# Last layer of heads of a four-layer kernel: the rotated rows moved by small transfers from ScalarE in place of swap products on TensorE, and the products half a product further ahead

## What is computed

```python
h = rmsnorm(x, attn_norm[layer])                  # x: 256 x 1024
proj = h @ w_in_odd[i]                            # 1024 x 3072
mq, mk, mv = jnp.split(proj, 3, axis=-1)          # each 16 heads of 64
mq = apply_partial_rope(mq.reshape(B, S, 16, 64), cos, sin)
mk = apply_partial_rope(mk.reshape(B, S, 16, 64), cos, sin)
moba_out = moba_attention(mq, mk, mv)             # softmax(causal(q k^T / 8)) v, per head
x = x + moba_out.reshape(B, S, 1024) @ w_out_odd[i]

def apply_partial_rope(t, cos, sin):              # rotates the first 16 of 64 features
    half = 8
    t1, t2 = t[..., :8], t[..., 8:16]
    rot = concatenate([t1 * cos - t2 * sin, t2 * cos + t1 * sin])
    return concatenate([rot, t[..., 16:]])
```

## Time and profile before

| | us |
|---|---|
| Three runs, median (lowest to highest) | 1150.59 (1150.18 to 1150.71) |
| The profiled execution, its time | 1150.78 |
| The profiled execution, its span | 1148.9 |
| TensorE busy (matmuls) | 1133.4, 99% |
| Weight loads of TensorE busy | 963.1, 84% |
| VectorE busy | 829.4, 72% |
| ScalarE busy | 654.8, 57% |
| GpSimd busy | 130.8, 11% |
| Traffic | 206.55 MB, 180 GB/s in the mean |

### The profile page before, as it was taken

One profiled execution on the slowest core, in us unless ns is written; L12 is line 12 of the kernel. 1 busy time (PEld: TensorE's weight loads), 2 busy tenths in 40 slices (PEclk: granted clock), 3 DMA queues, 4 the chain that ended last, 5 costly groups with the idle time before them and its releaser, 6 DMA issues.

```text
span 1148.9 us, 26306 instructions
## 1 busy us (share of the span) xinstructions
PE 1133.4 (99%) x10447; PEld 963.1 (84%) x10447; DVE 829.4 (72%) x1345; ACT 654.8 (57%) x1026; POOL 130.8 (11%) x168
## 2 busy tenths in 40 slices
PE   9999999999999999999999999999999999999998
PEld 7768888888888888888877788888877678888887
DVE  7787976655677987555669869776666666978664
ACT  7675666434567575523475767564455665755432
POOL 0000200000203200000243310000125431000010
PEclk9999999999999999999999999999999999999999
DMA  8752376555463375565353446654664344665461
GB/s 343 264 202 77 124 242 195 198 185 189 158 238 103 112 253 202 183 216 179 123 214 111 148 145 226 214 163 149 201 246 157 126 147 151 239 203 176 152 185 52
DMA packets 31466, 206.55 MB, mean 180 GB/s; under 512 B 3488, under 2 KB 3872, under 8 KB 10144
## 3 DMA queue, kind: packets, MB, share of 16 engines
q1 hardware_dynamic: 31104, 205.00, 52.3%
q10 hardware_dynamic: 288, 0.52, 0.1%
HBM read 204.46 MB, written 1.05 MB: 179 GB/s over the span
## 4 chain that ended last, share of the span: by engine, by line
PE 88%; DVE 9%; ACT 1%; issue 1%; DVEq 0%
PE ps L642 21%; PE ps L644 21%; PE ps L643 20%; DVE w_lo L2371 1%; PE ps L997 1%; PE ps L905 1%; PE ps L906 1%; PE ps L907 1%; PE ps L1497 1%; PE ps L1499 1%; PE ps L1498 1%; DVE m L2431 1%; PE ps L865 1%; PE ps L893 1%; PE ps L881 1%
## 5 line engine op out<-in xcount | busy, mean ns | idle before, releaser
L1580 ACT ACTIVATE w_hi<-staged 128x2048 f16<-128x2048 f32 (+3 forms) x191 | 338.1, 1786 | 230.6 <-PE ps L644 222.0
L643 PE MATMUL ps<-f_lo,w_hi 128*128 128x256 f16 x1588 | 432.8, 273 | 0.0
L644 PE MATMUL ps<-f_hi,w_lo 128*128 128x256 f16 x1588 | 432.8, 273 | 0.0
L642 PE MATMUL ps<-f_hi,w_hi 128*128 128x256 f16 x1588 | 432.8, 273 | 0.0
L2371 DVE SCALAR_TENSOR_TENSOR w_lo<-staged,w_hi 128x2048 f16<-128x2048 f32 (+3 forms) x191 | 406.7, 2141 | 27.0 <-ACT w_hi L1580 26.7
L642 PE MATMUL ps<-x_hi,w_hi 128*128 128x256 f16 x672 | 183.3, 273 | 0.0
L644 PE MATMUL ps<-x_hi,w_lo 128*128 128x256 f16 x672 | 183.2, 273 | 0.0
L643 PE MATMUL ps<-x_lo,w_hi 128*128 128x256 f16 x672 | 183.2, 273 | 0.0
L643 PEld LDWEIGHTS ps<-f_lo,w_hi 128*128 128x128 f16 x1588 | 155.4, 98 | 18.9
L642 PEld LDWEIGHTS ps<-f_hi,w_hi 128*128 128x128 f16 x1588 | 155.5, 98 | 18.1 <-issue 0.2
L644 PEld LDWEIGHTS ps<-f_hi,w_lo 128*128 128x128 f16 x1588 | 155.4, 98 | 18.1
(11 more groups left out here) (392 smaller groups left out, 1806.2 us busy)
## 6 DMA issues: line engine op xcount, KB each, us to landing
staged<-weights SPq DMA_DIRECT2D x165, 1024.0 KB, 5.0
staged<-weights SPq DMA_DIRECT2D x32, 704.0 KB, 4.2
xn<-bands SPq DMA_DIRECT2D x3, 512.0 KB, 10.1
m<-bands SPq DMA_DIRECT2D x3, 512.0 KB, 8.3
cst<-constants SPq DMA_DIRECT2D x1, 1027.0 KB, 7.7
h<-x_turned SPq DMA_DIRECT2D x2, 512.0 KB, 4.7
staged<-weights SPq DMA_DIRECT2D x2, 512.0 KB, 7.0
qT<-bands SPq DMA_DIRECT2D x2, 512.0 KB, 11.5
```

The lines of the kernel that those rows point to most:

```text
L642: pe.matmul(out, wh, xh[:, c, :], start=(c == 0), stop=False)
L643: pe.matmul(out, wh, xl[:, c, :], start=False, stop=False)
L644: last = pe.matmul(out, wl, xh[:, c, :], start=False, stop=(c == kc - 1))
L1580: act.activation(w_hi[:, s, o:o + n], staged[:, s, o:o + n], ACT.Copy, scale=SW).then_inc(hi_split, 1)
```

## The change

The rows that the rotation needs are no longer brought to their place by TensorE. ScalarE, after it has evicted the key of pair p, waits for its own evictions and issues four transfers within SBUF of 8 partitions x 2 KB (16 KB each: for each of the two heads and each of the two groups of 8 features, query and key together), from `raw_tile(p)` to `swapped_tile(p)`, which lies in `m`. VectorE's rotation reads this tile in place of PSUM and waits for the four transfers of its pair. The rows that are not rotated stay what they were in `m`, and are multiplied by zero sines.

The order is written anew. With p counting as before:

- TensorE, for p of 0 to 6: second half of (p+1,0), whole (p+1,1), scores p, turn p-1, first half of (p+2,0) (at p = 4 one value product, at p = 6 products of the output matrix), output product p-1 (at p = 4 then the other value product).
- ScalarE, for p of 0 to 7: evict (p,1), four transfers, split (two halves at p = 5 and 7), copy turned p-2, exponentials p-1, high part p-2, evict (p+1,0). At p = 5 the two values are evicted before and after the high part.
- VectorE, for p of 0 to 7: maxima p-1, rotation p, split one half, reciprocal p-1, low part p-2, second split where there is one.

GpSimd's order stays. To have two semaphores for the transfers, the three of the first model are made one, `latent_terms`, with the same increments in the same order.

```diff
--- before.py
+++ after.py
@@ -120,7 +120,7 @@
 
 VALUES_AFTER = 4
 
-ODD_SPLITS = ((4, 5), (4, 6), (6, 7), (8, 8), (10, 9), (16, 12), (18, 13, 14))
+ODD_SPLITS = ((4, 5), (4, 6), (6, 7), (8, 8), (10, 9), (14, 10, 11), (16, 12), (18, 13, 14))
 
 OUT_BANKS = (0, 1, 2, 4, 5, 6, 0, 1)
 
@@ -440,6 +440,7 @@
         p_lo_ready = [sem(f"p_lo_ready_{i}") for i in range(2)]
         down_taken = [sem(f"down_taken_{i}") for i in range(2)]
         swapped = sem("swapped")
+        rows_swapped = (sem("rows_swapped_0"), sem("rows_swapped_1"))
         turned = sem("turned")
         tables = sem("tables")
         sines = sem("sines")
@@ -467,11 +468,10 @@
             groups, heads, chunks = BEFORE[kind]
             return {s: chunks if s in ("o_hi", "o_lo") else heads if s == "peak" else groups for s in A}
 
-        eps_terms = sem("eps_terms")
-        latent_variance = sem("latent_variance")
+        latent_terms = sem("latent_terms")
+        LATENT_TERMS = {"eps": 2, "kv_norm": 3, "key": 4, "q_norm": 5}
         latent_rows = sem("latent_rows")
         latent_row_copied = sem("latent_row_copied")
-        key_scaled = sem("key_scaled")
 
         def mla_terms(hd, t):
             n = P * (t + 1)
@@ -520,6 +520,14 @@
         ROPE_AT = {"mla": 0, "even": 5, "odd": 11}
 
         ODD_ROWS = 15
+
+        def swapped_tile(p):
+            return m[:, 4 * (p % 2):4 * (p % 2) + 2, :]
+
+        def rope_half(r, h):
+
+            at = HD * r + ROPE2 // 2 * h
+            return slice(at, at + ROPE2 // 2)
 
         def added_before(name):
 
...
@@ -1500,16 +1508,6 @@
                 if end == DC:
                     last.then_inc(product["odd"], 1)
 
-            def swap_pair(p):
-
-                pe.wait_ge(drained["odd"], odd_at(p, 1) + 1)
-                if p:
-                    pe.wait_ge(turned, ROPE_AT["odd"] + p)
-                for which in range(2):
-                    last = pe.matmul(ps[:, 2, T * which:T * which + T], k("swap2"), raw_tile(p)[:, which, :], start=True,
-                                     stop=True)
-                last.then_inc(swapped, 1)
-
             pe.wait_ge(h_ready["down_0"], 2 + DC - 1)
             values(0, 0, normed("attn_1"))
             sums("attn_1")
@@ -1518,29 +1516,30 @@
             for which in range(2):
                 pair_product(0, which, 0, DC)
             last_pair = MOBA_HEADS // 2 - 1
+            pair_product(1, 0, 0, DC // 2)
             for p in range(last_pair):
-                pair_product(p + 1, 0, 0, DC // 2)
-                swap_pair(p)
-                pair_product(p + 1, 0, DC // 2, DC)
-                pair_product(p + 1, 1, 0, DC // 2)
+                pair_product(p + 1, 0, DC // 2 if p != VALUES_AFTER + 1 else 0, DC)
+                pair_product(p + 1, 1, 0, DC)
                 score_pair("moba", p)
                 if p:
                     turn_pair("moba", p - 1)
-                pair_product(p + 1, 1, DC // 2, DC)
+                if p == VALUES_AFTER:
+                    values(1, 0)
+                elif p + 2 <= last_pair:
+                    pair_product(p + 2, 0, 0, DC // 2)
+                else:
+                    arrived(2 * FIRST["outo"])
+                    pe.wait_ge(drained["odd"], 20)
+                    behind_pairs("moba", (0, 1), 0, 2)
                 if p:
                     out_pair("moba", p - 1)
                 if p == VALUES_AFTER:
-                    for t in range(TT):
-                        values(1, t)
-
-            arrived(2 * FIRST["outo"])
-            pe.wait_ge(drained["odd"], 20)
-            behind_pairs("moba", (0, 1), 0, 3)
-            swap_pair(last_pair)
-            behind_pairs("moba", (0, 1), 3, 4)
+                    values(1, 1)
+
+            behind_pairs("moba", (0, 1), 2, 5)
             score_pair("moba", last_pair)
             turn_pair("moba", last_pair - 1)
-            behind_pairs("moba", (0, 1), 4, 6)
+            behind_pairs("moba", (0, 1), 5, 6)
             out_pair("moba", last_pair - 1)
             pe.wait_ge(turned, ROPE_AT["odd"] + last_pair + 1)
             ended_pairs("moba", last_pair)
...
@@ -2177,9 +2176,16 @@
             def raw(p, which):
 
                 if p >= 2:
-                    act.wait_ge(swapped, ROPE_AT["odd"] + p - 1)
+                    act.wait_ge(turned, ROPE_AT["odd"] + p - 1)
                     act.wait_ge(normed_rows, ODD_ROWS + 2 * (p - 1))
                 odd_evict(odd_at(p, which), raw_tile(p)[:, which, :])
+                if which:
+
+                    act.wait_ge(drained["odd"], odd_at(p, 1) + 1)
+                    for r in range(P // HD):
+                        for e in range(2):
+                            act.dma_start(swapped_tile(p)[rope_half(r, e)], raw_tile(p)[rope_half(r, 1 - e)]).then_inc(
+                                rows_swapped[p % 2], 16)
 
             def split_after(done, *halves):
 
@@ -2194,26 +2200,21 @@
             raw(0, 0)
             split_after(2, 4)
             last_pair = MOBA_HEADS // 2 - 1
-            ODD_SPLITS = ((4, 5), (4, 6), (6, 7), (8, 8), (10, 9), (16, 12), (18, 13, 14))
-            for p in range(last_pair):
-                if p != VALUES_AFTER + 1:
-                    raw(p, 1)
-                    if p >= 2:
-                        high_pair("moba", p - 2)
+            for p in range(last_pair + 1):
+                raw(p, 1)
                 split_after(*ODD_SPLITS[p])
-                raw(p + 1, 0)
+                if p >= 2:
+                    turned_pair("moba", p - 2)
                 if p:
-                    turned_pair("moba", p - 1)
-                if p == last_pair - 1:
-                    raw(last_pair, 1)
-                exp_pair("moba", p)
-                if p == VALUES_AFTER:
-                    raw(p + 1, 1)
-                    high_pair("moba", p - 1)
-                    split_after(14, 10, 11)
-                    for t in range(TT):
-                        values(1, t)
-            high_pair("moba", last_pair - 2)
+                    exp_pair("moba", p - 1)
+                if p == VALUES_AFTER + 1:
+                    values(1, 0)
+                if p >= 2:
+                    high_pair("moba", p - 2)
+                if p == VALUES_AFTER + 1:
+                    values(1, 1)
+                if p < last_pair:
+                    raw(p + 1, 0)
             split_after(20, 15)
             turned_pair("moba", last_pair - 1)
             exp_pair("moba", last_pair)
...
@@ -3082,34 +3083,24 @@
 
             def rope_pair(p):
 
-                dve.wait_ge(swapped, ROPE_AT["odd"] + p + 1)
-                chain(dve.tensor_tensor(tmp[:, 2:4, :], ps[:, 2, :].rearrange("p (b t) -> p b t", b=2),
-                                        tmp[:, 1:2, :].to_broadcast([P, 2, T]), ALU.mult))
+                dve.wait_ge(rows_swapped[p % 2], 4 * 16 * (p // 2 + 1))
+                chain(dve.tensor_tensor(tmp[:, 2:4, :], swapped_tile(p), tmp[:, 1:2, :].to_broadcast([P, 2, T]), ALU.mult))
                 dve.wait_ge(normed_rows, ODD_ROWS + 2 * (p + 1))
                 dve.tensor_tensor(pair_tile(p), pair_tile(p), tmp[:, 2:4, :], ALU.add).then_inc(turned, 1)
 
             split(2 * u0 + 4)
             last_pair = MOBA_HEADS // 2 - 1
-            for p in range(last_pair):
-                if p and p != VALUES_AFTER + 1:
+            for p in range(last_pair + 1):
+                if p:
+                    reduce_pair("moba", p - 1)
+                rope_pair(p)
+                split(2 * u0 + ODD_SPLITS[p][1])
+                if p:
                     invert_pair("moba", p - 1)
-                    if p >= 2:
-                        low_pair("moba", p - 2)
-                rope_pair(p)
-                if p < last_pair - 1:
-                    for g in ODD_SPLITS[p][1:]:
-                        split(2 * u0 + g)
-                reduce_pair("moba", p)
-                if p == VALUES_AFTER:
-                    invert_pair("moba", p)
-                    low_pair("moba", p - 1)
-                    split(2 * u0 + 10)
-                    split(2 * u0 + 11)
-            split(2 * u0 + 13)
-            invert_pair("moba", last_pair - 1)
-            low_pair("moba", last_pair - 2)
-            rope_pair(last_pair)
-            split(2 * u0 + 14)
+                if p >= 2:
+                    low_pair("moba", p - 2)
+                for g in ODD_SPLITS[p][2:]:
+                    split(2 * u0 + g)
             reduce_pair("moba", last_pair)
             split(2 * u0 + 15)
             low_pair("moba", last_pair - 1)
```

More of the change, by code:

```diff
@@ L1162, in _ @@
                     pe.wait_ge(rooted, NORM_AT["kv_norm"])
-                    pe.wait_ge(eps_terms, len(LATENT))
+                    pe.wait_ge(latent_terms, LATENT_TERMS["eps"])
                     latent_sums("kv_norm")
@@ L1181, in _ @@
                     pe.wait_ge(latent_row_copied, 1)
-                    pe.wait_ge(key_scaled, 1)
+                    pe.wait_ge(latent_terms, LATENT_TERMS["key"])
```

(10 more changed lines are left out.)

## The result

The changed kernel takes 1174.22 us (median of 4 runs, 1172.82 to 1178.32) against 1150.65 for the kernel before (4 runs): 1.021 times the old time, 95% interval 1.0197 to 1.0222. It is slower by 23.6 us, where 6.9 were forecast and the range ended at 1166. The profiled execution took 1172.82 us with a span of 1170.9, 22.0 more than the old span.

A forecast was written before the change was run, and what follows sets the result against it. TensorE, busy 99% of the span, was taken as the bound. Start +1.5, steady pairs +3.2, value-product stretch -0.9 and end +3.1 summed to +6.9 us on the median of 1150.59: 1157.5 us, range 1147.5 to 1166.

The forecast's parts named there:

- The main mechanism: Steady pairs: ScalarE's issues and split precede the copy, so the output product waits 1.95 us; period 9.76, 1.08 longer.
- GpSimd's divide beside the split at the end: Stage's end: the divide begun at 8.6 nearly stands still beside split 14 and ends near 12.6.
- I take 0.43: ScalarE's time per transfer issue, 0.43 us, 1.72 for four per pair; bounds nothing and 0.48.
- the steady pair's wait of 1.95: Output product due at 2.97 us after the scores begins near 4.92, waiting for ScalarE's copy.
- The wait of turn 0: Stage's start: turn 0, due at 881.5, waits 2.7 us for the divide, over at 884.2.
- that of turn 6: Stage's end: turn 6 waits 2.2 us for GpSimd's divide, held beside split 14.
- the landing: Transfers' time from issue to arrival before the rotation: 2.8 us taken, bounds nothing and 5.0.
- rival 4: Transfers queue behind weight loads and land 5.0 us after issue: 1168.5 us; chance 0.09.
- rival 5: Waits let TensorE's clock fall; seven products at half level cost 18.3 us more: 1176 us; chance 0.03.
- the forecast's own signs of being wrong: No wait at the output product, a rotation wait over 5 us from issue, or clock below 1.00 between 862 and 966.
- Rival 2: Issuing costs ScalarE nothing: output product waits 0.2 us, period 8.0, total 1148.9 us; chance 0.15.
- Rival 3: All is covered, no wait at the output product, swaps and old waits gained: 1142.3 us; chance 0.13.

The follow-up runs named there:

- none: The changed kernel without its four transfers per pair and the wait for them, the rotation reading rows never brought: 1149.97 us, ratio 0.9993.
- warm: The changed kernel with idle matmuls on TensorE where it waits for the copy or the first rotation: 1169.22 us, ratio 1.0162.
- two_of_four: The changed kernel with only two of the four transfers per pair: 1157.43 us, ratio 1.0056.
- from_sp: The changed kernel with the same four transfers per pair issued by SyncE in place of ScalarE: 1159.64 us, ratio 1.0075.
- forms: The changed kernel with two transfers per pair within SBUF, their partitions varied from 4 to 128, rows not swapped: 1162.13 us, one run.
- forms_hbm: The changed kernel with two transfers per pair of varied partitions, from HBM in six pairs and SBUF in pairs 0 and 4: 1159.07 us, one run.
- sp_end_order: Against sp_reordered, one split fewer on ScalarE and VectorE ahead of pair 5's copy and pair 6's divide: 1146.74 us, ratio 0.9968.
- sp_reordered: The changed kernel with transfers from SyncE, pair 0's ahead of the next load, and VectorE's split and reciprocal before the rotation: 1152.11 us, ratio 1.0012.

## Why the prediction was wrong

**The main mechanism was the forecast one.** ScalarE's issues and split stand ahead of the copy; output products wait in pairs 1, 2 and 4, and longest in pair 5 (4.7 us for 3.7). The rest of the reckoning held too. For issues at no cost it gave a period of 8.0 and 1148.9 us, and `none` measured 7.97 and 1149.97. GpSimd's divide beside the split at the end, reckoned to take about 4, took 3.95 in the changed kernel. The 0.7 us of a cosine alone, which the earlier trace rows does not show, is 0.73 in the trace of before. Two steps failed, a term that was too small and one that the sum left out.

**Mis-sized: the issue, "I take 0.43".** It measured 0.66 from start to start, outside the bounds of nothing to 0.48. I had the bounds from transfers between HBM and SBUF; the change's are within SBUF, a form that the trace before did not have, and the upper bound should have been wider for it. With 2.65 us for four in place of 1.72, the steady pair's wait of 1.95 becomes 2.9 (2.94 measured) and each of the long waits grows by 0.9. Waits forecast at 15.4 us in sum were 21.5. The wait of turn 0 (2.7 forecast, 0.6 measured) and that of turn 6 (2.2 forecast, none measured) nearly went, because TensorE was by then later itself. In their place the output products of pairs 0 and 3, for which the forecast had no wait, waited 2.2 and 0.9 us; the first scores waited 4.0 and not 1.0. That the sum of the waits missed by 6.1 only is in part luck.

**Mis-sized: the landing, at the start only.** 2.8 us were taken. It was 4.7 for pair 0, beside a weight load, 3.0 for pair 2, beside the end of one, and 1.96 to 2.0 for pairs 3 to 7. That is the case of rival 4, at the start and not in every pair.

**Wrong: the clock, at nothing in the sum and rival 5 at 0.03.** It is the larger half of the miss: 5.0 us at the least by `warm`, about 8.7 by the balance, of 16.7. The waits make 6.1 of it; most of the rest is that the median lies 1.4 us above the profiled execution. The rival's own price was 18.3 on top of the forecast; it came for about half of that. I called it unlikely because the stage's row stood at 1.00, but no row before had an idle stretch like the ones that the forecast itself brought in. A forecast of seven waits of 1 to 3.7 us in 75 us should have carried the clock with it. Of the forecast's own signs of being wrong, this one came: a granted clock below 1.00 between 862 and 966 us.

Rival 2 falls by `two_of_four`: issues on ScalarE do cost it their time. The figure cited from the Trainium skill (DMA: Bandwidth & Descriptors, section Anatomy of one DMA, about 50 ns to dispatch, told of GpSimd's path) does not hold for ScalarE's queue: an issue took 0.30 us at the least, and 0.63 in the change. Rival 3 (all is covered) falls with the result, and even `none` does not reach its 1142.3.

## What to carry to other kernels

A transfer that replaces work on the busiest engine is not free on the engine that issues it: four issues here were 2.65 us of ScalarE's program, and everything behind them moved. Put them on a queue that has nothing urgent behind it, ahead of loads whose own wait comes later, and look at which buffer copy or divide is due within the same microseconds. When a forecast contains repeated waits of TensorE, price its clock with them; here the wait of 2.94 us in pair 1 cost 4.7 with the clock behind it, and the waits of the stage, 21.5 us, cost 30 in sum.

## What the runs showed of the hardware

- Within SBUF an issue of 16 KB takes 0.63 to 0.67 us on ScalarE's queue (the stage's first 1.23) and 0.62 to 0.79 on SyncE's (`from_sp`); with 4 to 128 partitions of 2 KB it takes 0.54 to 0.95 (`forms`). From HBM it takes 0.30 to 0.51 on ScalarE's queue in the same stage (`forms_hbm`), though up to 0.67 on SyncE's in the first 7 us of the kernel.
- 16 KB within SBUF land 1.96 us after issue when no load is in flight, and 2.9 to 5.0 when one is (5.0 in `warm`).
- In the changed kernel the granted clock fell behind five of TensorE's six waits of 2.2 to 4.7 us (to 0.50 to 0.74 in the lowest stretch of 5 us behind each) and stayed at 1.00 behind the sixth, 2.94 us long. Idle matmuls in those waits brought it to 1.00 and made the kernel 5.0 us faster. In `sp_end_order` a wait of 1.8 us had 0.83 over 10 us behind it.
- GpSimd's divide of two heads took 1.90 us in the old kernel's steady pairs, 2.70 beside VectorE's rotation in those of `sp_end_order`, 3.95 to 4.04 beside VectorE's split of weights (two inputs in SBUF) in the changed kernel, and 4.76 beside both in `sp_reordered`. The Trainium skill, SBUF — State Buffer, section Summary: rules for kernel authors, says that where a VectorE instruction has two SBUF inputs and one of GpSimd reads SBUF, the one that comes second waits until the other is done; the trace agrees: of the 4.76, 2.86 are more than alone, and the split beside it took 2.36.
